# A two-block network on one core: the first modulation as products of padded vector columns, the rotary angles during a merge

## The reference, cut to what matters

```python
shift_x, scale_x, gate_x = jnp.split(jax.nn.silu(c) @ w_mod + b_mod, 3, axis=-1)
shift_c, scale_c, gate_c = jnp.split(jax.nn.silu(c_ctx) @ w_mod + b_mod, 3, axis=-1)
hx = rms_norm(xs, norm_g) * (1 + scale_x[:, None]) + shift_x[:, None]
hc = rms_norm(cs, norm_g) * (1 + scale_c) + shift_c
px = split_cols(hx @ w_in + b_in)
```

## Time and profile before

| | |
|---|---|
| median of 3 runs | 3467.3 us |
| the profiled execution's own time | 3470.32 us |
| its span | 3468.4 us |
| TensorE products busy | 3241.9 us (93%) |
| VectorE, ScalarE, GpSimd busy | 1270.7, 829.1, 1437.1 us |
| granted TensorE clock, mean | 0.963 |

### The profile page before, as it was taken

How to read it: one execution, slowest core, us unless ns; L and a number is a source line. 1 busy time by engine, 2 the same in 40 slices (tenths; PEclk the granted TensorE clock), 3 DMA queues, 4 the chain that set the end, 5 groups by cost and what they waited for, 6 DMA issues and landing times.

```text
span 3468.4 us, 38766 instructions
## 1 busy us (share of the span) xinstructions
PE 3241.9 (93%) x14557; PEld 2219.7 (64%) x14557; DVE 1270.7 (37%) x2414; ACT 829.1 (24%) x1453; POOL 1437.1 (41%) x1372
## 2 busy tenths in 40 slices
PE   5999997899999999898999989999999999999997
PEld 5576565655665546465544438888995488889943
DVE  5112414634433222325544443434332334443322
ACT  2322324521111032314411112232211023222110
POOL 0489987000000049970000017777560177775600
PEclk6999998999999999999999989999999999999998
DMA  6111110013223111110045512122222222222221
GB/s 199 49 37 37 31 37 13 1 57 95 89 93 103 27 61 49 43 37 25 25 151 182 176 52 74 62 74 68 71 70 61 63 74 64 71 74 74 69 53 37
DMA packets 259180, 236.50 MB, mean 68 GB/s; under 512 B 20870, under 2 KB 257202, under 8 KB 258996
## 3 DMA queue, kind: packets, MB, share of 16 engines
q1 hardware_dynamic: 258996, 234.02, 22.1%
HBM read 231.90 MB, written 2.10 MB: 67 GB/s over the span
## 4 chain that ended last, share of the span: by engine, by line
PE 85%; DVE 7%; POOL 3%; ACT 3%; issue 2%; DMA 0%; DVEq 0%; ACTq 0%; SPq 0%; POOLq 0%
PE ps L426 38%; PE ps L963 22%; PE ps L456 11%; PE ps L1007 2%; DVE arena L1485 2%; ACT arena L1099 2%; PE ps L684 1%; PE ps L442 1%; PE ps L1051 1%; DVE small L1667 1%; POOL arena L1989 1%; DVE arena L1489 1%; PE ps L1043 1%; PE ps L572 1%; PE ps L715 1%
## 5 line engine op out<-in xcount | busy, mean ns | idle before, releaser
L426 PE MATMUL ps<-hT,wring 128*128 128x512 f32 (+1 forms) x1568 | 577.6, 529 | 0.4 <-ACT arena L1099 0.4
L426 PE MATMUL ps<-arena,wring 128*128 128x512 f32 (+1 forms) x1280 | 491.5, 544 | 10.3 <-DVE arena L1485 10.2
L2025 POOL TENSOR_TENSOR arena<-wring 128x512 f32<-128x512 f32 x72 | 92.8, 1289 | 928.2 <-DMA wring<-in_w_in 615.7
L426 PEld LDWEIGHTS ps<-hT,wring 128*128 128x128 f32 x1568 | 302.6, 195 | 256.2 <-issue 240.4
L1989 POOL TENSOR_TENSOR arena<-arena,posi 128x512 f32<-128x512 f32 (+1 forms) x360 | 410.8, 1141 | 30.0
L456 PE MATMUL ps<-hT,wring 128*128 128x512 f32 (+1 forms) x1088 | 403.5, 526 | 0.2
L426 PEld LDWEIGHTS ps<-arena,wring 128*128 128x128 f32 x1280 | 243.2, 191 | 247.0 <-issue 228.2
L1099 ACT ACTIVATE arena<-ps 128x256 f32<-128x256 f32 (+4 forms) x407 | 182.6, 449 | 706.3 <-PE ps L426 305.6
L1099 ACT ACT_TABLE_LOAD x152 | 195.0, 1283 | 533.5 <-PE ps L534 97.8
L456 PEld LDWEIGHTS ps<-hT,wring 128*128 128x128 f32 x1088 | 206.1, 194 | 168.4 <-issue 159.4
L1485 DVE TENSOR_TENSOR arena<-arena 128x768 f32<-128x768 f32 (+7 forms) x121 | 157.7, 1303 | 322.4 <-ACT arena L1099 319.1
(11 more groups left out here) (187 smaller groups left out, 4189.2 us busy)
## 6 DMA issues: line engine op xcount, KB each, us to landing
wring<-in_w_in SPq DMA_DIRECT2D x128, 1024.0 KB, 5.3
wring<-in_w_mod SPq DMA_DIRECT2D x24, 1024.0 KB, 7.8
wring<-in_w_out SPq DMA_DIRECT2D x24, 1024.0 KB, 5.6
wring<-in_w_ada SPq DMA_DIRECT2D x24, 1024.0 KB, 5.2
wring<-in_w_conv_out SPq DMA_DIRECT2D x8, 512.0 KB, 6.2
wring<-in_w_gla_out SPq DMA_DIRECT2D x8, 512.0 KB, 4.9
wring<-in_w_attn_out SPq DMA_DIRECT2D x8, 512.0 KB, 5.9
arena<-in_x SPq DMA_DIRECT2D x1, 2048.0 KB, 9.8
```

The source lines that it names most:

```text
L426: last = eng.matmul(o_(out), a, b_, start=(i == 0), stop=(i == len(parts) - 1))
L2025: pool.link(eng.tensor_tensor(t1, w[:, 0:4, P:2 * P], w[:, 0:4, 0:P], ALU.subtract))
```

## The change

1. **Padded vector columns.** All eight groups go to TensorE, the scale groups first. A tile `cpad` (128 x 8 x 32) holds silu of c and c_ctx in columns 0 and 1 and zeros in the other 30. It is the loaded operand, and the weights move: for each k one product of 32 loaded and 256 moving columns, to the 32 partitions 32q of a bank, q = k mod 4. ScalarE copies the bank (`mod_rows`); a second product per 128 columns with a two-column selector (K_MS) sums the four quarters and turns the rows into columns; VectorE adds b_mod.
2. **Order.** The square sums go out ahead of the eighth group; the shifts are added to the bias only after VectorE's scaling of x.
3. **Start.** The first constants are cut to 258 columns. Set 6 is loaded, turned and used first, the first four weights go ahead of set 0's rows, and all else (rest of the constants, sets 1 to 5, biases, gscan, rope) is issued by SyncE after the first layer's first weights (plan entry 8). Sets 1 to 5 are turned after the first z products. VectorE copies the context part of xT and squares the x part k by k; GpSimd squares the context part.
4. **Rotary.** The angles are computed in `rope` itself, with the positions' tile as scratch, ahead of the second quarter of the second layer's merge; the sines stand right behind this merge on ScalarE. The five memsets move behind the h sums of the second block.

```diff
-K_ID, K_ONE, K_HALF, ... = np.cumsum([0, 128, 128, 128, ...
+K_ID, K_ONE, K_MS, K_HALF, ... = np.cumsum([0, 128, 128, 2, 128, ...
+    c[0::32, K_MS] = 1.0
+    c[1::32, K_MS + 1] = 1.0
+FIRST_MODS = [4, 5, 6, 7, 0, 1, 2, 3]
...
             eng.wait_ge(*at("const in"))
+            eng.wait_ge(*at("c rows in"))
+            turn_rows([6])
             eng.wait_ge(m.sem("x_in"), 16 * 2)
...
             eng.wait_ge(*at("first rows in"))
-            turn_rows(FIRST_SETS)
+            turn_rows([0])
+            def first_mod(g):
+                w = weights(wv(I["w_mod"][0], g * 256, 256), KD, 256)
+                eng.wait_ge(*at(("c padded",)))
+                key = ("mod row", g)
+                b = next_bank("A", key)
+                for half in range(2):
+                    for q in range(4):
+                        last = eng.matmul(bank[b][32 * q:32 * q + 32, 0:256], cpad[:, 4 * half + q, :], w[:, 4 * half + q, :],
+                                          start=(half == 0), stop=(half == 1))
+                last.then_inc(*pe.tell(("full", key)))
+                used(("full", key))
+            def first_mod_columns(part):
+                def mms(o_):
+                    for g in FIRST_MODS[4 * part:4 * part + 4]:
+                        for j in range(2):
+                            f = 2 * (g % 4) + j
+                            last = eng.matmul(o_[:, 2 * f:2 * f + 2], mod_rows[:, g, j * P:(j + 1) * P], const[:, K_MS:K_MS + 2],
+                                              start=True, stop=True)
+                    return last
+                for g in FIRST_MODS[4 * part:4 * part + 4]:
+                    eng.wait_ge(*at(("free", ("mod row", g))))
+                job("V", ("mod columns", part), mms)
...
-                    for g in range(0, 8, 2):
-                        mod_load(0, g + 1)
-                        modulate(0, [g])
-                        mod_finish(0, g + 1)
-                    eng.wait_ge(*at("rows in"))
-                    turn_rows(LATER_SETS)
-                    claim(4, 5)
-                    square_sum(0)
+                    for i, g in enumerate(FIRST_MODS):
+                        if i == 7:
+                            claim(4, 5)
+                            square_sum(0)
+                            rings[0] = GLA_RINGS
+                        first_mod(g)
+                        if i == 4:
+                            first_mod_columns(0)
+                    first_mod_columns(1)
...
                 gla_gate(l, 0, 0)
                 pe.stage("proj1")
+                if l == 0:
+                    eng.wait_ge(*at("rows in"))
+                    turn_rows(LATER_SETS)
+                    eng.wait_ge(*at("all const in"))
                 tiles("val", l, wi, C_VAL, 2, segs(l))
```

ScalarE:

```diff
             evac(("cols", 6), cols[:, 6, :], 0, P)
             fn(cT[:, :], cols[:, 6, 8:32], ACT.Silu, ("cT",))
+            eng.wait_ge(*at(("c clear",)))
+            for c_ in range(2):
+                fn(cpad[:, :, c_], cT[:, 8 * c_:8 * c_ + 8], ACT.Copy, ("c padded",) if c_ else None)
+            for k in range(KD):
+                evac(("xT", k, "x"), xT[:, k, TC:T], 0, TX)
             evac(("cols", 0), cols[:, 0, :], 0, P)
+            for g in FIRST_MODS[:7]:
+                evac(("mod row", g), mod_rows[:, g, :], 0, 256)
...
+                if L == 0:
+                    evac(("mod row", FIRST_MODS[7]), mod_rows[:, FIRST_MODS[7], :], 0, 256)
+                    eng.wait_ge(*at(("first shifts",)))
...
                 gate_first(l, 0, 0)
                 act.stage("proj1")
+                for s in LATER_SETS if l == 0 else ():
+                    evac(("cols", s), cols[:, s, :], 0, P)
```

VectorE:

```diff
+            def first_mods(part):
+                f0 = 0 if part else 8
+                key = ("mod columns", part)
...
+                tt(modT[:, 0, f0:f0 + 8, :], bank_of[key][:, 0:16]..., cols[:, 0, 8 + f0:16 + f0]..., A_, ("free", key))
...
+                        cp(xT[:, k, 0:TC], bank_of[key][:, 0:TC], ("free", key))
+                        eng.wait_ge(*at(("free", ("xT", k, "x"))))
+                            tt(hT[:, k, TC:T], xk, xk, M_)
+                            tt(rstd[:, TC:T], rstd[:, TC:T], hT[:, k, TC:T], A_, ...)
...
                 for a in range(4):
+                    if l == DEPTH - 1 and a == 1:
+                        rotary_angles()
```

SyncE:

```diff
-            eng.dma_start(const[:, :], I["const"]).then_inc(m.sem("const_in"), 16)
+            eng.dma_start(const[:, 0:K_HALF], I["const"][:, 0:K_HALF]).then_inc(m.sem("const_in"), 16)
...
-            sig("first_rows_in", load_rows(FIRST_SETS, "first_rows_in"), "first rows in")
+            sig("c_rows_in", load_rows([6], "c_rows_in"), "c rows in")
             for n, (parts, _) in enumerate(plan[:RING]):
...
+            sig("first_rows_in", load_rows([0], "first_rows_in"), "first rows in")
...
+                if n == starts[0]:
+                    gate_weights(0)
+                    constants()
-                if n == starts[2]:
+                if n == merges[1]:
                     eng.wait_ge(*at(("conv", 1)))
                     eng.dma_start(posi[:, :], ...)
```

More of the change, by code:

```diff
@@ L340, in write_program @@
         landed = [0] * RING
-        starts, plan = [], []
+        starts, merges, plan = [], [], []
         mod_slot = {}
@@ L466, in tiles, with turn_rows @@
                     pass
+            def turn_rows(sets):
+                for s in sets:
+                    job("A", ("cols", s), lambda o_: eng.transpose(o_[:, 0:P], rows[:, s, :], ident))
             eng.wait_ge(*at("const in"))
+            eng.wait_ge(*at("c rows in"))
+            turn_rows([6])
             eng.wait_ge(m.sem("x_in"), 16 * 2)
@@ L1380, in _ @@
             act.stage("rotary")
[L1381 to L1384 removed]
+            eng.wait_ge(*at(("angles",)))
+            fn(rope[:, 1, :], rope[:, 1, :], ACT.Sin)
+            fn(rope[:, 0, :], rope[:, 0, :], ACT.Sin, ("rotary",))
             for l in range(DEPTH):
@@ L1524, in modulate @@
                 done.append((L, g))
+            def first_mods(part):
+                f0 = 0 if part else 8
+                key = ("mod columns", part)
+                eng.wait_ge(*at(("full", key)))
+                eng.wait_ge(*at(("free", ("cols", 0))))
+                tt(modT[:, 0, f0:f0 + 8, :], bank_of[key][:, 0:16].rearrange("p (a b) -> p a b", b=2),
+                   cols[:, 0, 8 + f0:16 + f0].unsqueeze(2).broadcast_to([P, 8, 2]), A_, ("free", key))
+                if part:
+                    m.mark(("first shifts",), *m.at[("free", key)])
             def norm(L):
@@ L1684, in attend, with rotary_angles @@
                 m.mark(("att out", l), *m.at[("free", ("o", first + len(pairs) - 1))])
+            def rotary_angles():
+                dve.stage("rotary")
+                eng.wait_ge(*at("positions in"))
+                C1, C2_, C3 = 6.28125, 0.0019350051879882812, 3.0199157663446332e-07
+                PI = float(np.nextafter(np.float32(np.pi), np.float32(0)))
+                zs, zc, turns = rope[:, 1, :], rope[:, 0, :], posi[:, :].bitcast(F32)
+                cp(zs, posi[:, :])
+                ts(zs, zs, const[:, K_FREQ:K_FREQ + 1], None, M_, None)
+                ts(turns, zs, float(1 / (2 * np.pi)), 12582912.0, M_, A_)
+                ts(turns, turns, -12582912.0, None, A_, None)
+                for c_ in (C1, C2_, C3):
+                    stt(zs, turns, -c_, zs, M_, A_)
+                ts(zs, zs, PI, -PI, ALU.min, ALU.max)
+                ts(zc, zs, HALF_PI, None, A_, None)
+                ts(turns, zc, PI, -2 * float(np.pi), ALU.is_gt, M_)
+                tt(zc, zc, turns, A_)
+                ts(zc, zc, PI, -PI, ALU.min, ALU.max, ("angles",))
             for l in range(DEPTH):
@@ L1711, in _ @@
                 dve.stage("rope")
+                eng.wait_ge(*at(("free", ("cols", l))))
+                ts(small[:, 20 + l:21 + l], col(l, QN), 0.125, None, M_, None)
                 eng.wait_ge(*at("rope in"))
@@ L1983, in _ @@
             pool = Lane(m, eng, "pool")
+            pool.stage("squares")
+            for k in range(KD):
+                eng.wait_ge(*at(("free", ("xT", k, "c"))))
+                xk, sums = xT[:, k, 0:TC], rstd[:, 0:TC]
+                pool.link(eng.tensor_tensor(sums if k == 0 else hT[:, k, 0:TC], xk, xk, ALU.mult))
+                if k:
+                    pool.link(eng.tensor_tensor(sums, sums, hT[:, k, 0:TC], ALU.add), ("squares", 0, "c") if k == KD - 1 else None)
             pool.stage("conv")
```

131 lines of the change are left out of this document (47 added, 84 removed).

## The result

The median fell from 3467.9 us (four runs, 3466.8 to 3470.8) to **3440.9 us** (four runs, 3440.1 to 3441.9): a ratio of 0.9918, 95% interval 0.9906 to 0.9930. That is 27.0 us of the medians; the two profiled executions, 3470.3 and 3440.1, differ by 30.2. The forecast was 3439.0 in a range of 3431 to 3455.

A forecast was written before the change was run, and what follows sets the result against it. TensorE's products, 85% of the last-ending chain, were taken as the bound, with gains only where TensorE idles or works slowly. Prologue 21.8 + rotary 6.6 = 28.4 us off 3470.3 gave 3441.9; median 3.0 lower, 3439; range 3431 to 3455.

The forecast's parts named there:

- I take that factor of two also for four tiles: Prologue's modulation groups: four tiles overlap only twofold, as two do; 1.73 us per group warm, 3.46 cold.
- Rival (1): Modulation groups: four tiles overlap fourfold, 0.9 us warm; weight slots bound, seventh group 2.5 us sooner, 3436 us; chance 0.15.
- Square sums to first product: Prologue, to the first product on h: old 9.3 us plus 5.6 for shifts waiting behind VectorE's eight scalings.
- Product stage: Prologue, products on h: follows ScalarE's adds, now end to end; 12.55 - 1.6 us, until 70.4.
- The new wait: After the z products: TensorE stalls 7.2 us for ScalarE's column copies behind the gate part; "val" 8.7 after z.
- the restart: After the stall behind z: the clock is low again, costing 1.5 us.
- the cover: SyncE's small transfers before the "val" weights: weights land near 65, wanted at 79.8, so 15 us to spare.
- rival (4): Small transfers take twice their time and hold the "val" weights until near 83, 3 us late: 3442 us; chance 0.07.
- Rotary: Second block's start: angles and sines leave the path, gap 14.5 to 8.4 us, product stage 9.36 to 8.84; saves 6.6.
- Rival (5): Second block: rotary part fails, gap stays at 14.5 us since the root waits for another thing; 3446 us; chance 0.05.
- (3): Modulation groups: neither tile overlap nor high clock, 6.9 us per group, square sums at 79.7, 3474 us; chance 0.04.
- Rival (2): Modulation groups: low clock or no overlap at high clock, 3.46 us each, seven end at 55.6; 3450 us; chance 0.17.

The follow-up runs named there:

- one tile: Changed kernel with all eight products of a modulation group on the same 32-column tile instead of four tiles: 3452.5 us (0.9952 of the kernel before).
- The kernel with two tiles: Changed kernel with the eight products of a modulation group alternating between two 32-column tiles instead of four: 3440.3 us (0.9919 of the kernel before).
- all three edits: Changed kernel with three groups among x's transposes, shifts ahead of scalings, and column copies ahead of the gate part: 3422.9 us (0.9860 of the kernel before).
- the kernel with the rows first: Changed kernel with set 0's 22 row transfers issued ahead of the first four weight loads: 3438.6 us (0.9914 of the kernel before).

## Why the prediction was right, and where it was wrong

- **Total.** 3439.0 forecast, 3440.9 measured, inside the range, on the side that had 0.93. The saving in the profiled executions was forecast at 28.4 and came out at 30.2.
- **Start of the first group**: forecast 27.7, measured 28.48. VectorE took 2.20 us per k, not 2.7: copy 0.42, square 0.69, sum 0.98, hand-overs the rest. I had counted with the 1.64 of the earlier trace rows. The rows landed at 27.65 (27 forecast).
- **The step that failed** is "I take that factor of two also for four tiles". The overlap is fourfold, 1.07 us for a group by itself and 0.9 in a row, not 1.73; cold 1.93, not 3.46. Rival (1) had that right. By the rule of the Trainium skill (TensorEngine Tiling (Array Packing), Performance Considerations), four times for 32 columns, a group in a row should by estimate cost a quarter of the 3.45 us on one tile, 0.86; the trace agrees, at 0.86 to 0.94. The "two-instruction products" that I held against it cost nothing.
- **That the number held is in part luck.** My forecast filled the time from 27.7 to 44.6 with work of TensorE, and no slot made it wait. Measured are 28.48 to 44.93, with 12.9 us of work and 3.5 of waits for weights. The products were shorter than I had said and the loads longer: the first slot came free at 30.38 (31.2 forecast), its load was in use 6.7 us later instead of 5.2, and the seventh group's 12.7 us later instead of 11.2. The kernel with two tiles is the one that I had forecast: 16.9 us of work and 0.4 of waits, and the same time as four.
- **Rival (1)'s time was wrong as well.** It let the seventh group end 2.5 us sooner than my forecast, at 42.1 (its own terms, a slot at 29.5, 11.2 us of loads and 0.9 for the group, give 41.6). It ended at 44.93: the slot came free 0.9 us later, the loads took 1.5 more, and the group 1.0 more, since the granted clock had fallen to 0.50.
- **Square sums to first product**: 14.9 forecast, 14.46 measured, and moving the shifts gave back 4.9 of the 5.6 us. **Product stage**: forecast to end at 70.4; 12.16 us long instead of 10.95, so at 71.5. The 1.6 us that I subtracted came to 0.4. The stage took 12.16 to 12.62 us in the kernels whose edits leave it alone. That the products now begin at a low clock (0.63 granted in the window from 50 to 60) may be why; no run tested it.
- **The new wait**: z to "val" 8.7 forecast, 8.64 measured; removing it gave 5.8, and the restart some 1.2 (1.5 forecast, a choice between 0.5 and 3). "val" at 79.8 forecast, 80.85 measured.
- **SyncE**: the "val" weights were to land near 65. They were only issued at 63.49, and the trace has the first landed at 70.5: the cover was 10.3 us, not 15. TensorE did not wait in the changed kernel, so rival (4) did not occur; with all three edits the cover was gone (issued at 58.16, landed at 64.8).
- **Rotary**: gap 8.4 forecast, 8.39 measured; product stage 8.84 forecast, 9.04 measured. 6.6 forecast; 6.4 in the traces, 6.7 and 8.8 by medians. The second quarter's merge did not slip. Rival (5) falls.
- **Rivals (2) and (3)** fall: the clock did rise with narrow tiles (1.00 from 36 to 44 us with two tiles). Rival (2)'s price was good, though: one tile, which is its case, put the square sums at 56.6 (55.6) and the time at 3452 (3450).

## What to carry to other kernels

A product of a padded vector with moving weights is cheap when its k parts share the array on several column tiles, but ask what feeds it: here two tiles did as well as four, since the next weights came no sooner. When the slowest engine of a hand-over is relieved, look at the order in front of the *next* one: three reorderings of a few lines, found as the releasers of the remaining idle times, were worth 16 us in the edited stages (18 by the medians), where the whole change had brought 27. And check which engine stands behind a short operation in a queue of long ones: 0.17 us of shifts behind 6.26 us of scalings cost 4.8.

## What was not expected of the hardware

- VectorE's sum of 512 columns took 0.98 us beside GpSimd's squares and sums of 256, not 0.69 and not 1.64, while its square of the same size beside them stayed at 0.69. GpSimd's own square of 256 columns took 0.61 by itself and about 1.0 beside VectorE.
- The granted clock doesn't fall at once with a wait. In the changed kernel the group behind 3.22 us without work still took 1.07 us; it fell in the 16 two-column products after it (2.86 us, against 1.95 in the kernel with the rows first), and the next group, with no wait before it, took 1.93 at a granted clock of 0.50 (41 to 43 us).
- Profiled executions differ by 3 to 7 us in stretches that no edit touches (2.7, 3.9 and 6.9 us above). For differences of that size the gap in the trace is the better measure, the median over several rounds the check on it.
